# The FFN of a decoder layer: full gate and up products become seven half products a pair, and the output projection keeps its sums in PSUM

## The reference

```python
f = x @ w_ffn_in[l]
ff = (jax.nn.silu(f[..., :FFN_HIDDEN]) * f[..., FFN_HIDDEN:]) @ w_ffn_out[l]
x = layer_norm(DN_ALPHA * x + ff, ln3_g[l], ln3_b[l])
```

## Time and profile before

| | |
|---|---|
| median of 3 runs | 2178.95 us (2177.84 to 2180.29) |
| profiled execution | 2180.05 us |
| its span in the profile | 2178.1 us |
| mean granted clock of PE | 0.979 of full |
| PE busy | 2059.9 us, 95% of the span, 10216 matmuls |
| POOL, DVE, ACT busy | 991.1, 825.3, 521.3 us |
| moved by DMA | 116.34 MB, mean 53 GB/s |

### The profile page before, as it was taken

The page is one execution under the profiler, slowest core; times in us unless marked ns, Lnnn a source line. Parts: engine busy times, 40 slices in busy tenths (PEclk is TensorE's granted clock), DMA queues, the critical chain, the costliest instruction groups (busy, mean ns, idle before and its releaser), DMA issues.

```text
span 2178.1 us, 25755 instructions
## 1 busy us (share of the span) xinstructions
PE 2059.9 (95%) x10216; PEld 1702.2 (78%) x10216; DVE 825.3 (38%) x839; ACT 521.3 (24%) x732; POOL 991.1 (46%) x497
## 2 busy tenths in 40 slices
PE   7999999999999999999889989899999999999995
PEld 6888888788777777877678877678888888888884
DVE  5647466300166656144553324542122212112115
ACT  2413224210154555110252221151100000000013
POOL 4232242333354445346775426763344433433375
PEclk9999999999999999999999999899999999999997
DMA  4021020112100000311211111101111111111112
...
DMA packets 33349, 116.34 MB, mean 53 GB/s; under 512 B 3728, under 2 KB 5136, under 8 KB 32272
## 3 DMA queue, kind: packets, MB, share of 16 engines
...
## 4 chain that ended last, share of the span: by engine, by line
PE 86%; DVE 8%; issue 2%; ACT 2%; POOL 1%; DMA 0%; POOLq 0%; DVEq 0%; ACTq 0%; SPq 0%
PE unit L437 23%; PE unit L443 23%; PE unit L441 23%; PE aux L602 2%; PE aux L608 2%; PE aux L606 2%; PE aux L415 2%; PE aux L417 1%; PE aux L416 1%; PE aux L562 1%; PE unit L551 1%; PE unit L415 1%; PE unit L417 1%; PE unit L416 1%; DVE ln_t L1483 1%
## 5 line engine op out<-in xcount | busy, mean ns | idle before, releaser
L280 POOL TENSOR_TENSOR w_hi<-w_raw,one 128x1024 fp32r<-128x1024 f32 (+1 forms) x130 | 245.1, 1885 | 888.7 <-PE unit L437 888.7
L437 PE MATMUL unit<-x_lo,w_hi 128*128 128x512 f32 x1440 | 563.3, 391 | 13.3 <-POOL w_lo L294 11.0
L443 PE MATMUL unit<-x_hi,w_lo 128*128 128x512 f32 x1440 | 561.3, 390 | 0.0
L441 PE MATMUL unit<-x_hi,w_hi 128*128 128x512 f32 x1440 | 561.1, 390 | 0.0
L437 PEld LDWEIGHTS unit<-x_lo,w_hi 128*128 128x128 f32 x1440 | 270.8, 188 | 72.5 <-POOL w_lo L294 11.0
L283 POOL TENSOR_TENSOR w_lo<-w_raw,w_hi 128x1024 fp32r<-128x1024 f32 (+1 forms) x130 | 322.1, 2478 | 10.2
L443 PEld LDWEIGHTS unit<-x_hi,w_lo 128*128 128x128 f32 x1440 | 270.7, 188 | 57.0
L441 PEld LDWEIGHTS unit<-x_hi,w_hi 128*128 128x128 f32 x1440 | 270.9, 188 | 55.5
L437 PE MATMUL unit<-a_lo,w_hi 128*128 128x512 f32 x608 | 240.2, 395 | 9.7 <-DVE a_lo L1395 9.7
L443 PE MATMUL unit<-a_hi,w_lo 128*128 128x512 f32 x608 | 239.2, 393 | 0.0
L441 PE MATMUL unit<-a_hi,w_hi 128*128 128x512 f32 x608 | 237.2, 390 | 0.0
...
## 6 DMA issues: line engine op xcount, KB each, us to landing
w_raw<-stream SPq DMA_DIRECT2D x156, 512.0 KB, 3.3
rope_sb<-rope ACTq DMA_DIRECT2D x8, 1024.0 KB, 6.8
...
acc<-xT ACTq DMA_DIRECT2D x8, 512.0 KB, 9.5
ret_branch<-acc ACTq DMA_DIRECT2D x8, 512.0 KB, 2.6
acc<-ret_branch ACTq DMA_DIRECT2D x8, 512.0 KB, 7.9
...
mem_raw<-memT ACTq DMA_DIRECT2D x1, 1024.0 KB, 5.4
```

What stands on the lines that cost most here:

```text
L280: pool.tensor_tensor(w_hi[s][:, 0:width], w_raw[:, s, 0:width], one[:].to_broadcast([P, width]), ALU.mult).then_inc(w_hi_done, 1)
L437: x = pe.matmul(out, w_hi[s][:, wk], lo[:, k, cols], start=first, stop=False, skip_group_check=True)
L441: pe.matmul(out, w_hi[s][:, wk], hi[:, k, cols], start=False, stop=False, skip_group_check=True)
L443: last = pe.matmul(out, w_lo[s][:, wk], hi[:, k, cols], start=False, stop=(k == kts - 1), skip_group_check=True)
```

## The change

**The products.** The gate tile p and the up tile p (rows) and their two halves of the 1024 input features (columns) make a 2 x 2 block matrix A. `x` has the same two halves of features (rows) and two halves of tokens (columns), B. Strassen's scheme in Winograd's form gets A times B from seven products of half size, each 4 blocks by 1 half by 3 pieces, 12 matmuls of 512 columns. They are A11 B11, A12 B21, S1 T1, S2 T2, S3 T3, S4 B22 and A22 T4, with S1 = A21 + A22, S2 = S1 - A11, S3 = A11 - A21, S4 = A12 - S2, and T1 = B12 - B11, T2 = B22 - T1, T3 = B22 - B12, T4 = T2 - B21. The T, which hold for all pairs, are made once at the end of norm 2 (`turn`, `turn_lo`); the S are made on DVE for each pair (`weight_sum`). The high piece of each half weight is now copied by ACT (`form_hi_part`), the low piece is made by POOL (`form_lo`), in a ring of four half slots. PE goes through them by `PRODUCTS`. S2 T2 is added in PSUM to A11 B11 and S3 T3 to both, after ACT has copied the bank as it stood (`held`); DVE adds up the four result blocks. Silu times up goes to `hidden`, and from there by DMA to `hidden_store` in DRAM.

**The output projection** has its own stage behind all products. It takes the tokens in three parts of 384, 384 and 256 columns (`PARTS`). In a part the eight output tiles lie in the eight PSUM banks, and PE goes over the 22 hidden tiles, 24 matmuls each: eight outputs by three pieces. The hidden tiles are loaded from DRAM and split again (`load_hidden`, `hidden_hi`, `hidden_lo`). Nine of the 22 output weights stay in SBUF after the first part (`KEPT`); the others are loaded and split in each part. The residual `x` comes back from `mid_x` in DRAM. The norm 3 of a part is done within the next part's tiles, at fixed tiles k, the last one behind the end.

Core of the diff:

```diff
+PRODUCTS = [(0, A11), (1, A11), (0, A12), (1, A12)] + [(p, i) for p in range(FFN_TILES)
+                                                       for i in range(2 if p < 2 else 0, 7)]
...
+PARTS = ((0, 384), (384, 384), (768, 256))
+KEPT = range(1, 18, 2)
+TILES = [(t, k) for t in range(len(PARTS)) for k in range(FFN_TILES)]
+OUT_SPLITS = [(t, k) for t, k in TILES if t == 0 or k not in KEPT]
...
         @block.sync
+            def load_out(m):
+                t, k = OUT_SPLITS[m]
+                if m >= 4:
+                    sp.wait_ge(w_split, CH_FFN + FORMS + m - 3)
+                sp.dma_start(out_raw(m), stream8[CH_FFN + 2 * FFN_TILES + k]).then_inc((o_loaded if m % 2 else w_loaded)[m // 2 % 2], 16)
+            def load_hidden(r):
+                t, k = TILES[r]
+                if r >= 2:
+                    sp.wait_ge(h_split, r - 1)
+                if t == 0:
+                    sp.wait_ge(hidden_stored[k % 2], 16 * (k // 2 + 1))
+                sp.dma_start(h_raw[:, r % 2, 0:PARTS[t][1]], hidden_store[k][:, columns(t)]).then_inc(h_loaded[r % 2], 16)
...
+            for p in range(FFN_TILES):
+                sp.wait_ge(w_split, CH_FFN + AT[p, S4] + 1)
...
+                sp.wait_ge(hidden_ready, 2 * p + 2)
+                sp.dma_start(hidden_store[p], hidden[:, p % 2, :]).then_inc(hidden_stored[p % 2], 16)
+            for r, (t, k) in enumerate(TILES):
+                if r >= 2:
+                    load_hidden(r)
+                if (t, k) in OUT_SPLITS and OUT_SPLITS.index((t, k)) + 4 < len(OUT_SPLITS):
+                    load_out(OUT_SPLITS.index((t, k)) + 4)
+                if (t, k) in ((0, 5), (0, 11), (2, 1)):
+                    load_residual({(0, 5): 0, (0, 11): 1, (2, 1): 2}[t, k])
...
         @block.gpsimd
+            def form_lo(f):
+                hi, lo = form_slot(f)
+                pool.wait_ge(w_hi_done, CH_FFN + f + 1)
+                pool.tensor_tensor(lo, form_source(*PRODUCTS[f]), f32(hi), ALU.subtract).then_inc(w_split, 1)
...
-            residual(n2, U_MO, CH_MO, False, D, True)
-            single(CH_FFN + 1)
-            normed_lo(n2, range(2 * KT))
-            split(CH_FFN + 2, 142 - CH_FFN - 2, 8 * P)
+            residual(n2, U_MO, CH_MO, False, D, False)
+            form_lo(0)
+            normed_parts()
+            for f in range(4, FORMS):
+                form_lo(f)
+            for m in range(len(OUT_SPLITS)):
+                out_lo(m)
...
         @block.tensor
+            def product(p, i):
+                pe.wait_ge(w_split, CH_FFN + AT[p, i] + 1)
...
+                if i == S2:
+                    pe.wait_ge(p1_held, p + 1)
...
+                for k in range(QUART):
+                    if p == 0:
+                        if i == S2:
+                            pe.wait_ge(t_split_pool, 2 * k + 2)
...
+                    product_part(p, i, k)
...
+            for r, (t, k) in enumerate(TILES):
+                n = PARTS[t][1]
+                if t and k == 7:
+                    y_stats(t - 1)
+                hi, lo = out_weight(t, k)
+                pe.wait_ge(w_split, CH_FFN + FORMS + splits_before(t, k))
+                pe.wait_ge(h_split, r + 1)
+                for o in range(KT):
...
+                    pe.matmul(out, hi[:, w], h_lo[:, r % 4, 0:n], start=k == 0, stop=False, skip_group_check=True)
...
+            y_stats(2)
...
         @block.scalar
+            def form_hi_part(f):
+                p, i = PRODUCTS[f]
+                if i in SUMS:
+                    act.wait_ge(form_summed, 4 * p + SUMS.index(i) + 1)
+                else:
+                    act.wait_ge(w_loaded[p % 2], 8 * CH_FFN + 32 * (p // 2 + 1))
+                if f < RING:
+                    act.wait_ge(unit_ready, U_MO + (7 if f < 2 else 8))
+                else:
+                    act.wait_ge(unit_ready, U_FFN + f - RING + 1)
+                act.activation(form_slot(f)[0], form_source(p, i), ACT.Copy).then_inc(w_hi_done, 1)
...
+            def hold_p1(p):
+                act.wait_ge(unit_ready, U_FFN + AT[p, A11] + 1)
+                if p:
+                    act.wait_ge(c11_done, p)
+                act.activation(held[:, 0, :], product_bank(p, A11), ACT.Copy).then_inc(p1_held, 1)
...
+            def out_hi(m):
+                t, k = OUT_SPLITS[m]
+                act.wait_ge((o_loaded if m % 2 else w_loaded)[m // 2 % 2], (0 if m % 2 else 8 * CH_FFN + 16 * FFN_TILES) + 16 * (m // 4 + 1))
+                if t == 0 and k:
+                    act.wait_ge(unit_ready, U_FFN + FORMS - (2 if k == 1 and k in KEPT else 0))
+                    if k in KEPT and KEPT.index(k) >= 6:
+                        for j in range(2):
+                            act.wait_ge(hidden_stored[j], 16 * FFN_TILES // 2)
+                if k not in KEPT and loose_index(t, k) >= W_FREE:
+                    wait_tiles(act, tile_done, unit_ready, loose_tile(loose_index(t, k) - W_FREE) + 1)
+                act.activation(out_weight(t, k)[0], out_raw(m), ACT.Copy).then_inc(w_hi_done, 1)
+            def hidden_hi(r):
+                n = PARTS[TILES[r][0]][1]
+                act.wait_ge(h_loaded[r % 2], 16 * (r // 2 + 1))
+                if r >= 4:
+                    wait_tiles(act, tile_done, unit_ready, r - 3)
+                act.activation(h_hi[:, r % 4, 0:n], h_raw[:, r % 2, 0:n], ACT.Copy).then_inc(h_hi_done, 1)
...
+            for f, (p, i) in enumerate(PRODUCTS):
...
+                if (p, i) == (1, A12):
+                    hold_p1(0)
+                if i == S2:
+                    hold_u2(p)
...
+                if f + RING < FORMS:
+                    form_hi_part(f + RING)
...
         @block.vector
+            def turn(k):
+                if k:
+                    turn_lo(k - 1)
+                dve.wait_ge(n2.affine, 10 + 2 * k)
+                b11, b21, b12, b22 = (acc[:, k + QUART * row, half(hf)] for hf in range(2) for row in range(2))
+                t1, t2, t3, t4 = (sum_slot(4 * k + j) for j in range(4))
+                for j, (out, l, r) in enumerate(((t1, b12, b11), (t2, b22, t1), (t3, b22, b12), (t4, t2, b21))):
+                    n = 4 * k + j
+                    if n >= 5:
+                        kk, jj = divmod(n - 5, 4)
+                        dve.wait_ge(t_split_dve if jj > 1 else t_split_pool, 2 * kk + jj % 2 + 1)
+                    if j in (1, 3):
+                        dve.wait_ge(t_ready, 4 * k + (1 if j == 1 else 2))
+                    dve.tensor_tensor(out, l, r, ALU.subtract).then_inc(t_ready, 1)
+            def turn_lo(k):
+                for j in (2, 3):
+                    dve.wait_ge(t_hi_done, 4 * k + j + 1)
+                    dve.tensor_tensor(t_lo[j + 1][:, k, :], sum_slot(4 * k + j), f32(t_hi[j + 1][:, k, :]), ALU.subtract
+                                      ).then_inc(t_split_dve, 1)
+            def weight_sum(p, j):
+                n = 16 + 4 * p + j
+                if n - 5 < 16:
+                    kk, jj = divmod(n - 5, 4)
+                    dve.wait_ge(t_split_dve if jj > 1 else t_split_pool, 2 * kk + jj % 2 + 1)
+                else:
+                    pp, jj = divmod(n - 21, 4)
+                    dve.wait_ge(w_split, CH_FFN + AT[pp, SUMS[jj]] + 1)
+                s1, s2 = form_source(p, S1), form_source(p, S2)
+                a11, a12, a21, a22 = (raw(p)[:, row, half(col)] for row in range(2) for col in range(2))
+                if j == 0:
+                    dve.wait_ge(w_loaded[p % 2], 8 * CH_FFN + 32 * (p // 2 + 1))
+                if j in (1, 3):
+                    dve.wait_ge(form_summed, 4 * p + (1 if j == 1 else 2))
+                out, l, r, op = ((s1, a21, a22, ALU.add), (s2, s1, a11, ALU.subtract),
+                                 (form_source(p, S3), a11, a21, ALU.subtract),
+                                 (form_source(p, S4), a12, s2, ALU.subtract))[j]
+                dve.tensor_tensor(out, l, r, op).then_inc(form_summed, 1)
...
-            layer_norm(n2, False, inverted_at=6)
+            for q, (hf, k) in enumerate(NORM_ORDER):
...
+                if q in (11, 13, 15):
+                    turn((q - 11) // 2)
+            turn(3)
+            turn_lo(3)
...
+            dve.wait_ge(mid_stored, 16 * 2 * KT)
+            dve.wait_ge(n2.done, len(NORM_PARTS))
+            for f, (p, i) in enumerate(PRODUCTS):
+                if (p, i) == (1, A12):
+                    for j in range(4):
+                        weight_sum(0, j)
+                    sum_c11(0)
...
+            for o in range(KT):
+                y_sum(2, o)
+            y_sum_chunks(2)
+            y_sum_squares(2)
+            y_total_lo_parts(2)
+            y_copy_square(2)
+            y_variance(2)
+            y_center(2, 0)
+            y_center(2, 1)
+            y_invert(2)
+            for o in range(KT):
+                if o >= 2:
+                    y_center(2, o)
+                y_scale(2, o)
```

621 lines of the change are left out of this document (530 added, 91 removed).

## The result

The changed kernel takes **2223.64 us** (median, 2221.22 to 2225.56) against 2178.93 for the kernel before beside it: ratio 1.0204, 95% interval 1.0187 to 1.0222. It is 2% slower; the forecast was 2163 us with a range up to 2187. The profiled execution has a span of 2222.6 us, where the sum stood at 2162.5 (2164.4 less the 1.95 around the span). So 60.1 us are to be found.

The account below looks back on a forecast made before the run. PE's matmuls were taken to bound the FFN; -59.8 + 7.7 + 3 + 32.4 + 2.6 + 8 - 9.6 = -15.7 from 2180.05 gave 2164.4, and 2163 us as median. Own range 2153 to 2174; 8 in 10, 2138 to 2187.

Parts of the forecast that it names:

- Part 4: Feeding the output tiles: two tiles cost 8.5 us, even with PE's 4.2 each; residual loads delay; +8, bounds 0 and 30.
- Part 2: Output projection: same columns in 1584 matmuls instead of 1056, +7.7 us; norm sums on PE between tiles, +3.
- The forecast's own sign: First token part of the output projection: forecast wrong if a tile there takes over 4.6 us.
- Rival B: Output feed: SP's queue sets the first token part's pace, 5.3 us a tile, +31 for +8; time 2186; chance 0.15.
- Part 3: Seam from second norm into products: PE restarts at 1467.0 instead of 1434.6, +32.4 us; low clock afterwards, +2.6.
- the shorter lead of the norm: Seam: norm starts about 3.5 us earlier, but its twelfth scaling comes at about 1430.6, not 1429.2.
- the middle course for collisions: Seam: colliding DVE and POOL steps take 1.7 us together, restart 1467; bounds 1459 without collisions, 1482 with all.
- Part 1: Products: 1848 matmuls of 512 columns instead of 2112, 264 less x 0.2267, -59.8 us; feeding them costs nothing.
- C: Products: half weights come late, 0.3 us for each of 154 products, 46 us; time 2209; chance 0.06.
- D: Output projection: narrower matmuls go by the weight load, costing 37 and 14 us; time 2214; chance 0.04.
- Part 5: Last tile matmul to the end: 21.5 us against 31.1, -9.6; bounds -13 and -3.
- A: Cheap seam, restart 1459 (-8), no waits in output tiles (-8), end at lower bound (-3.4); time 2144; chance 0.27.

Follow-up runs that it names:

- The mended order: Changed kernel, two hidden buffers, hidden tile r+1 instead of r put into SP's queue in step r: 2173.64 us, ratio 0.9974.
- the run with the early sums: Changed kernel with T1 and T2 low parts on DVE, plus weight sums S1 and S2 of pair 0 made before the T: 2213.9 us, ratio 1.0168.
- the place mended: Changed kernel with 160 unused bytes a partition behind inv_col: 2205.25 us, ratio 1.0127.
- The shift of 32 bytes: Kernel before with 32 unused bytes a partition behind its constants, as inv_col shifts buffers in the changed kernel: 2187.66 us, ratio 1.0038.
- distance 96: Blocks a, ret, sbo begin 96 bytes modulo 256 from the weights' place, as in the unpadded changed kernel: 2223.64 us.
- distance 0: Blocks a, ret, sbo begin at the weights' place modulo 256; changed kernel with 160 bytes of padding 2205.25 us, kernel before with 192 bytes 2174.86.

## Why the prediction was wrong

**Part 4 is the step that failed.** It put +8 (bounds 0 and 30) on the feed of the output tiles, and Part 2 +3 on the sums between them; they cost 59.9 over the columns. The sums themselves are 2.6 of these (12 matmuls, 1.3 us, in each of two parts), so the feed cost 57. The working of one turn was nearly right: 8.5 us for two tiles foreseen, 8.11 measured, against PE's 8.4. What I drew from it was wrong. "Even with PE's pace" I took for nearly free; it means that the feed has no lead, and then each disturbance reaches PE in full and none is made up. The tile times show it: 11 us in the first part behind its start and the two residual loads, 7 at the change to the second part (2 at the next), where DVE's first addition stands behind the low part of a tile that came late, 10 and 19 at the tiles around the reductions and the copy of the mean, 9 in the last tiles of the third part. The forecast's own sign, a tile of the first part over 4.6 us, is there in 7 of 22, the longest 9.5. The mended order, with the same work on every engine, takes 257.1 us where I had forecast 258.1.

**Rival B** named the place, SP's queue, and its time, 2186, was nearer than mine, but not its price: the turn was not 5.3 a tile in the first part, and 43 of the 60 us fell into the second and third parts, which B left out and of which I named only the reductions, without a price of their own. It had 0.15. Rows of the order were enough to see it: a hidden load behind a wait for the next weight.

**The reductions** were mis-sized: 5.67 for 3.6. The earlier trace rows has a reduction over neighbouring elements of PSUM; these step 1536 bytes from element to element in SBUF. The Trainium skill (SBUF — State Buffer, "Door 1: The DMA port swizzle") says that accesses within the same 16 bytes run at the full rate and each crossing to another line pays. By these rows it is 1.85 ns an element against 1.20, and the trace agrees in kind. The two rows differ in the memory as well as in the step, and no run separates these.

**Part 3** came out to the tenth: 65.5 us from mem_o's end to PE's restart, both forecast and measured, and not by luck alone: counted from mem_o's end the last step of each of the four blocks, the last low part and the two weight sums lie within 1.3 us of the forecast's times. So the shorter lead of the norm and the middle course for collisions were right. Single steps show both sides; DVE in the seam, alone and beside POOL:

```profile
1438.45 0.68 DVE L2049 TENSOR_TENSOR sums_a<-acc 128x512 f32<-128x512 f32 x1
1439.05 1.75 DVE L2049 TENSOR_TENSOR sums_b<-sums_a,acc 128x512 f32<-128x512 f32 x1
```

The releaser was the forecast one, too, ACT's copy of the bank behind three weight copies. What the forecast didn't see is that this copy would have held PE without the weights, as the run with the early sums shows. And I had treated the seam as given; 11.5 us of it came off by moving low parts from POOL to DVE and two sums and a copy forward.

**Part 1**: the count was right and the products do keep PE fed (1.00 clock, no halts). The 7.6 us too much are the place of the T blocks, 7.5 by the distances; with the place mended the stretch is 410.5, forecast 410.7. C falls. **Part 2**: 384 columns kept 0.175 and 256 columns took 0.120 for 0.118, and the sums 2.6 for 3, so D falls. **Part 5**: 23.4 for 21.5, the two reductions being 2.6 longer than their sizing (2.3 each, itself less than the 2.45 of its own rate). The **7 us ahead of the seam** no step had. The shift of 32 bytes accounts for up to 6.0 by 1344 matmuls x 0.0045, but in this trace only 1.6 of the 7 lie in mem_o and 2.0 ahead of cross-attention; the other 3.4 lie in cross-attention, within what profiles of the same code differ by, and their cause stays open. On average mem_o ends at 1406.2 in the nine profiles at distance 96 and at 1399.9 in the four at distance 0, so the place as a whole is worth some 6 us there, where 9.0 were expected for going to distance 0. A's time, 2144, is reached in the end, but by other means than A had: order, place and a mended seam.
